# New order of loads, strips, Toeplitz transfers and input products in the state-space stage of a hybrid trunk

## Chip, cores and metric

One NeuronCore of a Trainium2 chip runs the whole program, in float32. The metric is the device time of one execution in microseconds (us), median of the runs; lower is better.

## What is computed

Two layers on a sequence of 512 frames of width 1024: an S5 layer (a diagonal complex state space in 64 groups of 16 channels with 64 states each, then a GLU), a SwiGLU network, a retention layer, another SwiGLU network and a last RMSNorm. The change lies in the first stage alone, which is this part of the reference:

```python
def s5_mixer(u, lam_re, lam_im, log_step, b_re, b_im, c_re, c_im, d, glu_w, glu_b):
    lam = lax.complex(lam_re, lam_im)
    lam_bar = jnp.exp(lam * jnp.exp(log_step)[:, None])
    b_bar = ((lam_bar - 1.0) / lam)[..., None] * lax.complex(b_re, b_im)
    bu = jnp.einsum('blgn,gpn->blgp', uf, b_bar)
    _, states = lax.associative_scan(_linear_recurrence_combine, (a, bu), axis=1)   # a: lam_bar
    y = jnp.einsum('gnp,blgp->blgn', c, states).real + d * uf
    y = jax.nn.gelu(y.reshape(bsz, seq, D_MODEL))
    return y * jax.nn.sigmoid(y @ glu_w + glu_b)

x = x + s5_mixer(rmsnorm(x, s5_norm[j]), ...)     # then: x = x + swiglu(rmsnorm(x), ...)
```

## The kernel before

The program is written out by hand for each engine: a stream of instructions for SyncE (SP), which issues DMAs, and for TensorE (PE), ScalarE (ACT), VectorE (DVE) and GpSimd (POOL), tied by semaphores. Each engine takes its own stream strictly in order, so an instruction that waits holds all that stand behind it. PSUM has eight banks. Each use of a bank is a "fill"; the list `S5_FILLS` (line 79) deals the fills of the stage to banks 4 to 7 in turn, and the consumers wait for `bank_full` and `bank_free` by it. ACT copies nearly every filled bank to SBUF.

The S5 stage works in chunks of 8 steps (64 chunks of 8 steps make the 512 frames; 32 pairs of groups, `J`).

1. SP loads the eigenvalues, B (`b_loaded`), the norm gain, C (`c_loaded`, eight DMAs, line 425), the gain and D on few partitions (`d_loaded`), and six vectors (`vecs_loaded`). ACT issues two DMAs of 1 MB each with x by chunks (`xc_loaded`, line 864).
2. DVE works out the eigenvalues and their powers 0 to 8 (`powers`), then the output powers `c_powers`. ACT copies the gained B into `fb` (four copies), squares the eight steps of x (line 880), takes the root, copies C out of PSUM and writes the normed x (`xn`, line 891).
3. `half_tables` (DVE, line 1248) makes eight half tables for the inputs, three operations of 1024 elements each; PE transposes each (`s5_tables`, line 506); ACT copies it out. PE transposes `xn` (`s5_steps`, line 558) and multiplies tables and inputs (`s5_inputs`, eight results `b`). ACT copies these into `states`.
4. POOL multiplies C by the powers into `r_tc`, seven blocks of it (`tc_ready`); DVE makes the eighth (`tc_last_ready`). From each, PE makes a strip of the convolution (`strips(k)`, line 570); ACT copies it into `strip`, which lies in the space of the raw weights (`w_raw`). DMAs shift copies of the strips into the Toeplitz matrices `toep` (`toeplitz_half(queue, part, half)`, line 389: eight DMAs each; four parts, each of two halves; part p needs strips 2p and 2p+1). Toeplitz memory is zeroed by ACT first.
5. DVE scans the states: within segments (`seg_done` 1), over the segments' carries (`seg_done` 2), and lifts them in four parts (`scan_done` 1 to 4).
6. SP loads x again by tokens (`x_tok`, 2 MB, line 441). PE transposes it to `xT` (line 609), which ACT copies out in eight tiles.
7. PE accumulates `y_inputs(k)` (Toeplitz matrix by inputs, line 639) and `y_states(k)` (line 620) in eight banks. ACT applies the GELU, PE transposes back (`y_transposed`), DVE and ACT copy and split into a high and a low part. The GLU's matmuls follow (lines 673 to 675), and with them the long rest of the program, in which PE is nearly always at work on weights that are split into `w_hi` (ACT) and `w_lo` (DVE).

In the kernel before, ACT issues the second halves of parts 1, 2 and 3, and SP the rest. ACT's split of the first GLU weights, `split_weights(0, 0)`, stands ahead of its eight DMAs of part 3. The PE stream of that point reads:

```python
            pe.wait_ge(seg_done, 2)
            for k in range(4):
                if k % 2 == 0:
                    pe.wait_ge(toep_loaded[k // 2], 16 * 2 * STEPS)
                y_inputs(k)
            strips(6)
            pe.wait_ge(toep_loaded[2], 16 * 2 * STEPS)
            y_inputs(4)
            y_inputs(5)
            keep_clock(s5_open("y", 6)[0], 8)
            for k in range(4):
                y_states(k)
            pe.wait_ge(toep_loaded[3], 16 * 2 * STEPS)
```

Of the kernel before, what the change touches and what calls it, by code (L numbers as in the profile page):

```python
# [30 lines left out]
ALU = mybir.AluOpType  # L31
ACT = mybir.ActivationFunctionType
# [45 lines left out]
SHARED = 4  # L78
S5_FILLS = [("bt", 0), ("bt", 1), ("lam", 0), ("ms", 0), ("vec", 0), ("ct", 0), ("ct", 1)]
S5_FILLS += [("tb", 0), ("tb", 1)] + [("u", k) for k in range(8)] + [("tb", 2), ("tb", 3)]  # L80
for _c in range(1, 4):
    S5_FILLS += [("tb", 4 * _c), ("tb", 4 * _c + 1), ("b", 2 * _c - 2)]
    if _c == 2:
        S5_FILLS += [("strip", 0)]
    S5_FILLS += [("tb", 4 * _c + 2), ("tb", 4 * _c + 3), ("b", 2 * _c - 1)]
S5_FILLS += [("b", 6), ("b", 7), ("strip", 1), ("strip", 7), ("strip", 2), ("strip", 3)]
S5_LATE = [("strip", 4), ("strip", 5), ("strip", 6)]
S5_AT, _used = {}, [0] * 8


def _place(fill, b):
    S5_AT[fill] = (b, _used[b])
    _used[b] += 1
# [8 lines left out]
for _kind in ("y", "yt"):  # L102
    for _k in range(8):
        _place((_kind, _k), _k)
PART = 2 * JB
# [52 lines left out]
def trunk(nc, x, s5_norm, lam_re, lam_im, log_step, b_re, b_im, c_re, c_im, s5_d, glu_w, glu_b,  # L158
          ret_norm, ret_w, ret_gn, ret_wo, ffn_norm, ffn_gate, ffn_up, ffn_down, final_norm,
          ident_in, rope_in, decay_in, out):  # L160
    with ExitStack() as ctx:
# [3 lines left out]
        def sem(name):  # L165
            return ctx.enter_context(nc.semaphore(name))
# [45 lines left out]
        tb = r_w[:, 1024:3072].rearrange("p (r a) -> p r a", r=2)  # L212
        tc_tmp = r_w[:, 0:512]
        prod = r_w[:, 2048:3072].rearrange("p (s a) -> p s a", s=2)
# [9 lines left out]
        rows = r_3[0:J, 4096:4096 + 28 * P].rearrange("p (s a) -> p s a", a=P)  # L224
        vec_rows = r_3[64:64 + NVEC, 4096:4096 + P]
        gain_wide = r_3[:, 8192 - J * N:8192]
# [92 lines left out]
        gain_loaded = sem("gain_loaded")  # L319
        ct_copied = sem("ct_copied")  # L320
        tc_last_ready = sem("tc_last_ready")
# [80 lines left out]
        def _(sp):  # L402
# [17 lines left out]
            for half in range(2):  # L420
                gain_half = s5_norm[0][half * J * N:(half + 1) * J * N]
                sp.dma_start(gain_wide[64 * half:64 * half + 64, :], gain_half.partition_broadcast(64)).then_inc(gain_loaded, 16)
            for ri, src in enumerate((c_re, c_im)):
                for b in range(4):
                    sp.dma_start(c_rows[:, ri, b, :].rearrange("m (h p) -> m h p", h=2),
                                 src[0].rearrange("(h b j) n p -> b (j n) h p", h=2, b=4)[b]).then_inc(c_loaded, 16)
# [5 lines left out]
            for col, vec in ((V_GLU_B, glu_b[0]), (V_RET, ret_norm[0]), (V_FFN0, ffn_norm[0]),  # L432
                             (V_FFN1, ffn_norm[1]), (V_FINAL, final_norm), (V_GN, ret_gn[0])):
                n = vec.shape[0] // P
                sp.dma_start(vec_rows[col:col + n, :], vec.rearrange("(k p) -> k p", p=P)).then_inc(vecs_loaded, 16)

            b, fill = S5_AT[("tb", 4 * NTAB - 1)]
            sp.wait_ge(bank_full[b], fill + 1)
            sp.wait_ge(tb_ready, 2 * NTAB)
            sp.wait_ge(tc_last_ready, 1)  # L440
            sp.dma_start(x_tok, x[0].rearrange("(t p) d -> p t d", p=P)).then_inc(x_loaded, 16)

            toeplitz_half(sp, 0, 0)
            toeplitz_half(sp, 0, 1)
            toeplitz_half(sp, 1, 0)
            toeplitz_half(sp, 2, 0)
            for part in range(2):
# [44 lines left out]
        def _(pe):  # L492
# [54 lines left out]
            pe.matmul(ps[:, 0:STEPS], pair, small[:, 0:STEPS], start=True, stop=True).then_inc(full, 1)  # L547
            ps, full = s5_open("vec", 0)
            pe.wait_ge(vecs_loaded, 6 * 16)
            pe.transpose(ps[:, 0:NVEC], vec_rows, ident[64:64 + NVEC, 64:64 + NVEC]).then_inc(full, 1)  # L550
            pe.wait_ge(c_loaded, 8 * 16)
# [12 lines left out]

            s5_tables(0, 0)
            pe.wait_ge(xn_ready, STEPS)
            for k in range(8):
                s5_steps(k)
            s5_tables(0, 1)
            def strips(k):  # L570
# [14 lines left out]
            for c in range(1, NTAB):  # L585
                s5_tables(c, 0)
                if c == 1:
                    for n in range(8):
                        b, fill = S5_AT[("u", n)]
                        pe.wait_ge(bank_free[b], fill + 1)  # L590
                s5_inputs(2 * c - 2)
                if c == 2:
                    pe.wait_ge(fb_ready, 4)
                    pe.wait_ge(diag_ready, 1)
                    strips(0)
                s5_tables(c, 1)
                s5_inputs(2 * c - 1)
            s5_inputs(NBLK - 2)
            s5_inputs(NBLK - 1)
            strips(1)  # L600
            strips(NBLK - 1)
# [37 lines left out]
            def y_inputs(k):  # L639
                s5_open("y", k)  # L640
                for jj, half, rows64, o in y_pairs(k):


                    pe.matmul(o, u[:, jj, half, :], toep[:, J * half + jj, :], start=(jj % 4 == 0), stop=False)

            pe.wait_ge(seg_done, 2)
            for k in range(4):
                if k % 2 == 0:
                    pe.wait_ge(toep_loaded[k // 2], 16 * 2 * STEPS)
                y_inputs(k)  # L650
            strips(6)
            pe.wait_ge(toep_loaded[2], 16 * 2 * STEPS)
# [189 lines left out]
        def _(act):  # L842
# [24 lines left out]
            act.activation(rows[:, 11, :], rows[:, 10, :], ACT.Sin).then_inc(sin_ready, 1)  # L867
            act.activation(rows[:, 12, :], rows[:, 10, :], ACT.Sin, scale=0.5).then_inc(sin_ready, 1)
            act.wait_ge(fb_zeroed, 1)
            for ri in range(2):  # L870
                b, fill = S5_AT[("bt", ri)]
                act.wait_ge(bank_free[b], fill + 1)
                for half in range(2):
                    rows64 = slice(64 * half, 64 * half + 64)
                    copy(fb[rows64, ri, :, N * half:N * half + N], bt_gained[ri][rows64]).then_inc(fb_ready, 1)
            act.wait_ge(xc_loaded, 32)
            for t in range(STEPS):
                if t:
                    act.wait_ge(ms_ready, t)
                act.activation(junk, xc[:, t, :], ACT.Square, accum_out=small[:, t:t + 1]).then_inc(ms_ready, 1)  # L880
            ps, free = s5_full("ms", 0)
            act.activation(small[:, 8:16], ps[:, 0:STEPS], ACT.Sqrt, bias=eps[:, :], scale=1.0 / D).then_inc(free, 1)
            ps, free = s5_full("vec", 0)
            copy(vecs[:, :], ps[:, 0:NVEC]).then_inc(free, 1)
            for ri in range(2):
# [32 lines left out]

            s5_table_out(0, 0)
            for k in range(8):  # L920
                s5_steps_out(k)
            s5_table_out(0, 1)
            for c in range(1, NTAB):
                s5_table_out(c, 0)
                s5_input_out(2 * c - 2)
                if c == 2:
                    strip_out(0)
                if c == NTAB - 1:
                    zero_toeplitz(2)
                s5_table_out(c, 1)  # L930
                s5_input_out(2 * c - 1)
                if c < NTAB - 1:
                    zero_toeplitz(c - 1)
                else:
                    act.wait_ge(tb_ready, 2 * NTAB)
                    for ri in range(2):
                        copy(ct_last[:, ri, :, :], ct[:, ri, J - JB:J, :]).then_inc(ct_copied, 1)
            s5_input_out(NBLK - 2)
            s5_input_out(NBLK - 1)
            strip_out(1)  # L940
            zero_toeplitz(3)
            strip_out(7)
            for k in range(4, 8):
                zero_toeplitz(k)
            strip_out(2)
            strip_out(3)
            toeplitz_half(act, 1, 1)
            for k in range(KT):
# [3 lines left out]
            strip_out(5)  # L952
            toeplitz_half(act, 2, 1)
            strip_out(6)
            split_weights(0, 0)
            toeplitz_half(act, 3, 1)
# [16 lines left out]
            for k in range(8):  # L973
                gelu(k)
                if k >= 5 and k % 2:
                    y_high((k - 5) // 2)
# [127 lines left out]
        def _(dve):  # L1104
# [115 lines left out]

            step(dve.memset(powers[:, 0, 0, :], 1.0))
            step(dve.memset(powers[:, 1, 0, :], 0.0))
# [13 lines left out]
            for have in (1, 2, 4):  # L1236
# [4 lines left out]

            t = [prod[:, i, :].rearrange("p (r k j) -> p r k j", r=2, k=STEPS) for i in range(2)]
            complex_mul([c_powers[:, i, :, :] for i in range(2)], powers[:, :, 0:STEPS, :],
                        [repeated(lam_t[:, 2 + i, :], 1, STEPS) for i in range(2)], t)
            dve.tensor_copy(seg_powers[:, :, 0, :], powers[:, :, STEPS, :]).then_inc(powers_ready, 1)
            dve.wait_ge(powers_ready, 1)

# [22 lines left out]

            dve.wait_ge(ct_copied, 2)
            js = slice(J - JB, J)
# [332 lines left out]
        def _(pool):  # L1605
# [19 lines left out]

            pool.wait_ge(powers_ready, 1)
            pool.wait_ge(d_loaded, 64)
            d_flat = d_diag[:, :, :].rearrange("p j n -> p (j n)")
# [81 lines left out]
```

## Time and profile before

| | |
|---|---|
| median of 3 runs | 1310.13 us (1308.87 to 1310.64) |
| the profiled execution | 1309.56 us, of which the span is 1307.8 us |
| PE busy | 1253.6 us |
| first GLU matmul (end of the S5 stage) | 123.5 us after the start of the span |

The span runs from the first to the last instruction; 1.8 us lie around it. All times below that look like "89.70" are us from the start of the span. A row of the timeline has start, duration, engine, line, operation, output and inputs, the count, and in brackets the idle time of that engine ahead of it with what ended it. "ACTq" and "SPq" are the queues in which these engines issue DMAs.

### The profile page before, as it was taken

To read this page: it belongs to the slowest core of one execution; us is meant where nothing else is said; L and a number is where in the kernel's file an instruction comes from. 1 tells how busy PE (TensorE), PEld (TensorE's weight loads), DVE (VectorE), ACT (ScalarE), POOL (GpSimd) and SP (SyncE) were. 2 spreads that over 40 slices of the span, in tenths; PEclk is the share of its full clock that TensorE was granted. 3 is DMA by queue.
4 is the path that set the end of the run, shared out by engine and by line. 5 is a ranking of instruction groups with operands and counts; after the bars stand their busy time and mean duration, and the time that the engine had idled before them with its cause. 6 is when DMAs were issued, how large, how long until landed. Compare 5 with 4: busy or idle time off the path is not lost.

```text
span 1307.8 us, 16043 instructions
## 1 busy us (share of the span) xinstructions
PE 1253.6 (96%) x6253; PEld 1039.9 (80%) x6253; DVE 694.8 (53%) x822; ACT 465.5 (36%) x481; POOL 58.1 (4%) x64
## 2 busy tenths in 40 slices
PE   2779999999999999999999999999999999999997
PEld 2768778888887888888888888888788888887886
DVE  8797874444444445555556464554355454444433
ACT  4834544242423333324223332332233232323222
POOL 2960000000000000000000000000000000000000
PEclk9989999999999999999999999999999999999999
DMA  5053323333322323322313223233332323222231
GB/s 112 2 136 100 96 88 105 96 96 96 96 86 81 96 88 114 103 100 96 105 33 121 79 65 103 65 96 96 97 97 88 104 90 102 90 72 89 88 101 73
DMA packets 147791, 119.18 MB, mean 91 GB/s; under 512 B 12857, under 2 KB 140017, under 8 KB 147761
## 3 DMA queue, kind: packets, MB, share of 16 engines
q1 hardware_dynamic: 143584, 115.78, 28.5%
q10 hardware_dynamic: 4176, 2.98, 1.1%
q8 instruction: 21, 0.34, 0.1%
q14 instruction: 10, 0.07, 0.0%
HBM read 114.29 MB, written 2.10 MB: 89 GB/s over the span
## 4 chain that ended last, share of the span: by engine, by line
PE 89%; DVE 4%; ACT 3%; issue 1%; DMA 1%; ACTq 1%; SPq 0%; DVEq 0%
PE bank L673 25%; PE bank L675 25%; PE bank L674 25%; PE bank L769 2%; PE bank L770 2%; PE bank L771 2%; PE bank L780 1%; ACTq L398 1%; DVE w_lo L1126 1%; PE bank L797 1%; PE bank L795 1%; PE bank L796 1%; DVE tmp L1116 1%; DMA w_raw<-in_s_glu_w_dram 1%; PE bank L625 1%
## 5 line engine op out<-in xcount | busy, mean ns | idle before, releaser
L673 PE MATMUL bank<-u_hi,w_hi 128*128 128x512 f32 x960 | 375.5, 391 | 2.0 <-DVE xT L1390 1.1
L675 PE MATMUL bank<-u_hi,w_lo 128*128 128x512 f32 x960 | 374.0, 390 | 0.0
L674 PE MATMUL bank<-u_lo,w_hi 128*128 128x512 f32 x960 | 373.8, 389 | 0.0
L1126 DVE TENSOR_TENSOR w_lo<-w_raw,w_hi 128x2048 fp32r<-128x2048 f32 x112 | 256.7, 2292 | 200.2 <-ACT w_hi L850 199.8
L850 ACT ACTIVATE w_hi<-w_raw 128x2048 fp32r<-128x2048 f32 x112 | 213.5, 1906 | 188.6 <-PE bank L675 146.4
L673 PEld LDWEIGHTS bank<-u_hi,w_hi 128*128 128x128 f32 x960 | 180.3, 188 | 40.5 <-issue 2.0
L675 PEld LDWEIGHTS bank<-u_hi,w_lo 128*128 128x128 f32 x960 | 180.3, 188 | 37.6
L674 PEld LDWEIGHTS bank<-u_lo,w_hi 128*128 128x128 f32 x960 | 180.3, 188 | 37.4 <-issue 0.5
L673 PE MATMUL bank<-h_hi,w_hi 128*128 128x512 f32 x352 | 137.3, 390 | 2.8 <-DVE w_lo L1126 2.8
L674 PE MATMUL bank<-h_lo,w_hi 128*128 128x512 f32 x352 | 137.1, 389 | 0.0
L675 PE MATMUL bank<-h_hi,w_lo 128*128 128x512 f32 x352 | 137.0, 389 | 0.0
L850 ACT ACTIVATE h_hi<-tmp 128x512 f32 x44 | 27.8, 632 | 234.3 <-DVE tmp L1116 234.3
L1116 DVE TENSOR_TENSOR tmp<-bank,tmp 128x512 f32<-128x512 f32 (+3 forms) x60 | 38.1, 635 | 98.9 <-PE bank L675 94.3
L983 ACT ACTIVATE tmp<-xT 128x512 f32 (+1 forms) x32 | 20.2, 633 | 183.4 <-DVE xT L1390 183.4
L673 PEld LDWEIGHTS bank<-h_hi,w_hi 128*128 128x128 f32 x352 | 66.1, 188 | 17.3 <-DVE w_lo L1126 3.6
L674 PEld LDWEIGHTS bank<-h_lo,w_hi 128*128 128x128 f32 x352 | 66.1, 188 | 13.7
L675 PEld LDWEIGHTS bank<-h_hi,w_lo 128*128 128x128 f32 x352 | 66.1, 188 | 13.6
L1390 DVE TENSOR_TENSOR xT<-bank,xT 128x512 f32 (+1 forms) x24 | 16.6, 692 | 96.5 <-PE bank L675 96.5
L1035 ACT ACTIVATE tmp<-tmp 128x512 f32<-128x512 f32 x44 | 27.8, 632 | 70.6 <-DVE tmp L1465 69.6
L1477 DVE TENSOR_TENSOR h_lo<-tmp,h_hi 128x512 f32 x44 | 30.5, 692 | 40.6 <-ACT h_hi L850 40.6
L673 PE MATMUL bank<-y_hi,w_hi 128*128 128x512 f32 x128 | 49.9, 390 | 0.0
L675 PE MATMUL bank<-y_hi,w_lo 128*128 128x512 f32 x128 | 49.8, 389 | 0.0
(199 smaller groups left out, 1352.2 us busy)
## 6 DMA issues: line engine op xcount, KB each, us to landing
w_raw<-in_ret_w_qkvg_dram SPq DMA_DIRECT2D x24, 1024.0 KB, 5.0
w_raw<-in_ffn_w_gate_dram SPq DMA_DIRECT2D x22, 1024.0 KB, 5.1
w_raw<-in_ffn_w_up_dram SPq DMA_DIRECT2D x22, 1024.0 KB, 5.1
w_raw<-in_ffn_w_down_dram SPq DMA_DIRECT2D x32, 704.0 KB, 4.2
w_raw<-in_ret_w_o_dram SPq DMA_DIRECT2D x8, 1024.0 KB, 5.1
w_raw<-in_s_glu_w_dram SPq DMA_DIRECT2D x4, 1024.0 KB, 6.0
s<-in_x_dram ACTq DMA_DIRECT2D x2, 1024.0 KB, 12.2
s_w<-in_x_dram SPq DMA_DIRECT2D x1, 2048.0 KB, 10.0
```

The source lines that it names most:

```text
L673: pe.matmul(o, w_hi[w][:, w_cols], hi, start=first, stop=False)
L674: pe.matmul(o, w_hi[w][:, w_cols], lo, start=False, stop=False)
L675: return pe.matmul(o, w_lo[w][:, w_cols], hi, start=False, stop=end)
L769: pe.matmul(o, a_hi, w_hi[s][:, cols], start=(kk == 0), stop=False)
L770: pe.matmul(o, a_hi, w_lo[s][:, cols], start=False, stop=False)
L771: mm = pe.matmul(o, a_lo, w_hi[s][:, cols], start=False, stop=(kk == KT - 1))
L850: return act.activation(o, i, ACT.Copy, scale=scale)
L983: act.activation(sq, tile(xT, t), ACT.Square).then_inc(sq_ready, 1)
L1035: act.activation(sig[:, m, :], sig[:, m, :], ACT.Silu).then_inc(gate_ready, 1)
L1116: return dve.tensor_tensor(o, a, b, ALU.mult)
L1126: dve.tensor_tensor(w_lo[s][:, :], w_raw[:, s, :], w_hi[s][:, :].bitcast(F32), ALU.subtract).then_inc(w_lo_ready[s], 1)
L1477: dve.tensor_tensor(tile(h_lo, i * 2 + m), act_raw[:, m, :], tile(h_hi, i * 2 + m).bitcast(F32), ALU.subtract).then_inc(h_split, 1)
```

## The change

It changes the order of work inside the S5 stage; nothing that is computed is left out or added.

- SP waits for x by chunks (`xc_loaded`) ahead of its loads of C; all that stands behind these waits too.
- ACT squares x ahead of its copies into `fb`.
- DVE no longer makes `c_powers` and the copy `seg_powers`; POOL does. DVE, not ACT, copies `ct_last`.
- PE transposes the half table (0,1) ahead of the eight transposes of `xn`; ACT's copies follow that order. Strip 1 comes after table 2 rather than after the last inputs; the vectors' transpose comes late.
- The load of x by tokens no longer waits for `tc_last_ready` (the buffer `tc_tmp` moved), but stands behind the 16 DMAs of Toeplitz part 0.
- SP issues parts 0, 1 and 2 whole and the first half of part 3; ACT only the second half of part 3.
- ACT's `split_weights(0, 0)` comes after its second GELU.
- `y_inputs(0)` and `(1)` take banks 2 and 3 and wait only for `seg_done` 1; strip 6 comes between them and `y_inputs(2)`.

```diff
-S5_FILLS = [("bt", 0), ("bt", 1), ("lam", 0), ("ms", 0), ("vec", 0), ("ct", 0), ("ct", 1)]
-S5_FILLS += [("tb", 0), ("tb", 1)] + [("u", k) for k in range(8)] + [("tb", 2), ("tb", 3)]
+S5_FILLS = [("bt", 0), ("bt", 1), ("lam", 0), ("ms", 0), ("ct", 0), ("ct", 1)]
+S5_FILLS += [("tb", k) for k in range(4)] + [("u", k) for k in range(8)]
...
+Y_BANK = [2, 3, 0, 1, 4, 5, 6, 7]
...
-        tc_tmp = r_w[:, 0:512]
+        tc_tmp = xT[:, 7, :]
...
+            sp.wait_ge(xc_loaded, 32)
             for ri, src in enumerate((c_re, c_im)):
...
+            toeplitz_half(sp, 0, 0)
+            toeplitz_half(sp, 0, 1)
+
             b, fill = S5_AT[("tb", 4 * NTAB - 1)]
             sp.wait_ge(bank_full[b], fill + 1)
             sp.wait_ge(tb_ready, 2 * NTAB)
-            sp.wait_ge(tc_last_ready, 1)
             sp.dma_start(x_tok, x[0].rearrange("(t p) d -> p t d", p=P)).then_inc(x_loaded, 16)
 
-            toeplitz_half(sp, 0, 0)
-            toeplitz_half(sp, 0, 1)
-            toeplitz_half(sp, 1, 0)
-            toeplitz_half(sp, 2, 0)
+            for part in range(1, NPART - 1):
+                for half in range(2):
+                    toeplitz_half(sp, part, half)
...
             s5_tables(0, 0)
+            s5_tables(0, 1)
             pe.wait_ge(xn_ready, STEPS)
             for k in range(8):
                 s5_steps(k)
-            s5_tables(0, 1)
...
+            pe.wait_ge(seg_done, 1)
+            pe.wait_ge(toep_loaded[0], 16 * 2 * STEPS)
+            y_inputs(0)
+            y_inputs(1)
+            strips(6)
             pe.wait_ge(seg_done, 2)
-            for k in range(4):
-                if k % 2 == 0:
-                    pe.wait_ge(toep_loaded[k // 2], 16 * 2 * STEPS)
-                y_inputs(k)
-            strips(6)
+            pe.wait_ge(toep_loaded[1], 16 * 2 * STEPS)
+            y_inputs(2)
+            y_inputs(3)
...
-            toeplitz_half(act, 1, 1)
             for k in range(KT):
...
             strip_out(5)
-            toeplitz_half(act, 2, 1)
             strip_out(6)
-            split_weights(0, 0)
             toeplitz_half(act, 3, 1)
...
                 gelu(k)
+                if k == 1:
+                    split_weights(0, 0)
...
             pool.wait_ge(powers_ready, 1)
+            b, fill = S5_AT[("lam", 0)]
+            pool.wait_ge(bank_free[b], fill + 1)
+            t = [xT[:, i, :].rearrange("p (r k j) -> p r k j", r=2, k=STEPS) for i in range(2)]
+            for i in range(2):
+                step(mul(t[i], powers[:, :, 0:STEPS, :],
+                         repeated(repeated(lam_t[:, 2 + i, :], 1, STEPS), 1, 2)))
+            settle()
+            step(pool.tensor_tensor(c_powers[:, 0, :, :], t[0][:, 0], t[1][:, 1], ALU.subtract))
+            pool.tensor_tensor(c_powers[:, 1, :, :], t[0][:, 1], t[1][:, 0], ALU.add).then_inc(c_powers_ready, 1)
```

## Rows read from the trace of the kernel before

**Rows 1.** The page's first part: busy time, share of the span, instructions of PE.

```profile
PE 1253.6 (96%) x6253; PEld 1039.9 (80%) x6253; DVE 694.8 (53%) x822; ACT 465.5 (36%) x481; POOL 58.1 (4%) x64
```

**Rows 2.** Chain that ended last, 60 to 125 us: start, duration, what.

```profile
89.70 0.56 SPq L398
...
94.90 7.79 DMA w_raw<-in_s_glu_w_dram
...
107.30 2.77 DMA s<-w_raw
```

**Rows 3.** Timeline of PE, 79 to 124 us.

```profile
79.67 4.90 PE L609 MATMUL bank<-ident,s_w 128*128 128x128 f32 x24 [2.99 <-ACT xT L850]
...
86.71 1.94 PE L578 MATMUL bank<-s_tc,s_fb 128*32 128x128 f32 x16
...
97.39 1.97 PE L644 MATMUL bank<-s,s_u 128*64 128x128 f32 x32 [1.62 <-DMA s<-w_raw]
...
101.27 7.53 PE L625 MATMUL bank<-s_tc,s_states 64*64 64x128 f32 x128
110.11 1.97 PE L644 MATMUL bank<-s,s_u 128*64 128x128 f32 x32 [1.31 <-DMA s<-w_raw]
...
123.53 0.48 PE L673 MATMUL bank<-g_hi,w_hi 128*128 128x512 f32 x1
```

**Rows 4.** Stretches: length, busy time of each engine, granted clock, DMA share, GB/s.

```profile
68.00:72.00 4.00, 3.95 (x45) 3.42 (x43) 3.86 (x5) 4.00 (x6) 3.76 (x5) 1.00 1.01 407
...
72.00:75.30 3.30, 0.00 (x0) 0.00 (x0) 3.16 (x5) 0.88 (x2) 3.22 (x3) 1.00 0.92 196
...
79.60:82.80 3.20, 3.13 (x14) 2.76 (x15) 3.10 (x4) 1.88 (x5) 3.04 (x4) 0.50 0.34 70
```

**Rows 5.** Line 864 (x by chunks), its landings; DMA queues of 16 to 19 us.

```profile
DMA to landing us min/median/max: 9.9/12.2/14.5
...
q1 hardware_dynamic: 1644, 0.42, 75.5%
q10 hardware_dynamic: 148, 0.27, 43.1%
```

**Rows 6.** The page's DMA issues (x by tokens); line 398, SP, 79 to 86 us.

```profile
s_w<-in_x_dram SPq DMA_DIRECT2D x1, 2048.0 KB, 10.0
...
L398 SPq DMA_DIRECT2D s<-w_raw x7: 600/605/611, 78.7 to 82.6; - x7
...
DMA to landing us min/median/max: 1.8/2.0/2.3
```

**Rows 7.** Timeline of ACT, 18 to 64 us.

```profile
18.57 2.44 ACT L850 ACTIVATE s_fb<-bank 64x512 f32<-64x512 f32 x4 [8.91 <-DVE bank L1116]
...
27.05 1.28 ACT L882 ACT_TABLE_LOAD   x1
...
30.45 5.00 ACT L891 ACTIVATE s<-s,small 128x512 f32<-128x512 f32 x8
...
60.93 1.97 ACT L850 ACTIVATE s_states<-bank 128x512 f32<-128x512 f32 x2
63.80 0.59 ACT L850 ACTIVATE w_raw<-bank 32x512 f32<-32x512 f32 x1 [0.89 <-PE bank L581]
```

**Rows 8.** Timeline of DVE, 22 to 67 us.

```profile
22.49 1.30 DVE L1116 TENSOR_TENSOR s_w<-s_powers,s_lam_t 128x512 f32<-128x512 f32 x2
...
24.84 1.23 DVE L1116 TENSOR_TENSOR bank<-bank,s_powers 128x1024 f32<-128x1024 f32 x1
...
41.63 1.22 DVE L1259 TENSOR_TENSOR s_w<-bank,s_w 128x1024 f32<-128x1024 f32 x1 [3.17 <-PE bank L513]
...
65.85 1.23 DVE L1116 TENSOR_TENSOR bank<-s_states,bank 128x1024 f32<-128x1024 f32 x1
```

**Rows 9.** Timeline of POOL, 30 to 87 us.

```profile
30.80 2.17 POOL L1616 TENSOR_TENSOR s_pool_tmp<-s_ct,s_c_powers 128x512 f32<-128x512 f32 x2
...
85.00 1.27 POOL L1670 TENSOR_TENSOR s_tc<-s_pool_tmp 128x512 f32<-128x512 f32 x1
```

More of the change, by code:

```diff
@@ L78 @@
 SHARED = 4
-S5_FILLS = [("bt", 0), ("bt", 1), ("lam", 0), ("ms", 0), ("vec", 0), ("ct", 0), ("ct", 1)]
-S5_FILLS += [("tb", 0), ("tb", 1)] + [("u", k) for k in range(8)] + [("tb", 2), ("tb", 3)]
+S5_FILLS = [("bt", 0), ("bt", 1), ("lam", 0), ("ms", 0), ("ct", 0), ("ct", 1)]
+S5_FILLS += [("tb", k) for k in range(4)] + [("u", k) for k in range(8)]
 for _c in range(1, 4):
[L82 to L86, printed above, removed]
+    for _h in range(2):
+        S5_FILLS += [("tb", 4 * _c + 2 * _h), ("tb", 4 * _c + 2 * _h + 1), ("b", 2 * _c - 2 + _h)]
+        if _c == 2:
+            S5_FILLS += [("strip", _h)]
+S5_FILLS += [("b", 6), ("b", 7), ("vec", 0), ("strip", 7), ("strip", 2), ("strip", 3)]
 S5_LATE = [("strip", 4), ("strip", 5), ("strip", 6)]
+Y_BANK = [2, 3, 0, 1, 4, 5, 6, 7]
 S5_AT, _used = {}, [0] * 8
@@ L103 @@
     for _k in range(8):
-        _place((_kind, _k), _k)
+        _place((_kind, _k), Y_BANK[_k])
 PART = 2 * JB
@@ L224, in trunk @@
         rows = r_3[0:J, 4096:4096 + 28 * P].rearrange("p (s a) -> p s a", a=P)
-        vec_rows = r_3[64:64 + NVEC, 4096:4096 + P]
+        vec_rows = xT[64:64 + NVEC, 6, 0:P]
         gain_wide = r_3[:, 8192 - J * N:8192]
@@ L319, in trunk @@
         gain_loaded = sem("gain_loaded")
-        ct_copied = sem("ct_copied")
+        c_powers_ready = sem("c_powers_ready")
         tc_last_ready = sem("tc_last_ready")
@@ L547, in _ @@
             pe.matmul(ps[:, 0:STEPS], pair, small[:, 0:STEPS], start=True, stop=True).then_inc(full, 1)
-            ps, full = s5_open("vec", 0)
-            pe.wait_ge(vecs_loaded, 6 * 16)
-            pe.transpose(ps[:, 0:NVEC], vec_rows, ident[64:64 + NVEC, 64:64 + NVEC]).then_inc(full, 1)
             pe.wait_ge(c_loaded, 8 * 16)
@@ L597, in _ @@
                 s5_inputs(2 * c - 1)
+                if c == 2:
+                    strips(1)
             s5_inputs(NBLK - 2)
             s5_inputs(NBLK - 1)
-            strips(1)
+            ps, full = s5_open("vec", 0)
+            pe.wait_ge(vecs_loaded, 6 * 16)
+            pe.transpose(ps[:, 0:NVEC], vec_rows, ident[64:64 + NVEC, 64:64 + NVEC]).then_inc(full, 1)
             strips(NBLK - 1)
@@ L868, in _ @@
             act.activation(rows[:, 12, :], rows[:, 10, :], ACT.Sin, scale=0.5).then_inc(sin_ready, 1)
+            act.wait_ge(xc_loaded, 32)
+            for t in range(STEPS):
+                if t:
+                    act.wait_ge(ms_ready, t)
+                act.activation(junk, xc[:, t, :], ACT.Square, accum_out=small[:, t:t + 1]).then_inc(ms_ready, 1)
             act.wait_ge(fb_zeroed, 1)
@@ L875, in _ @@
                     copy(fb[rows64, ri, :, N * half:N * half + N], bt_gained[ri][rows64]).then_inc(fb_ready, 1)
[L876 to L880, printed above, removed]
             ps, free = s5_full("ms", 0)
             act.activation(small[:, 8:16], ps[:, 0:STEPS], ACT.Sqrt, bias=eps[:, :], scale=1.0 / D).then_inc(free, 1)
-            ps, free = s5_full("vec", 0)
-            copy(vecs[:, :], ps[:, 0:NVEC]).then_inc(free, 1)
             for ri in range(2):
@@ L919, in _ @@
             s5_table_out(0, 0)
+            s5_table_out(0, 1)
             for k in range(8):
                 s5_steps_out(k)
-            s5_table_out(0, 1)
             for c in range(1, NTAB):
-                s5_table_out(c, 0)
-                s5_input_out(2 * c - 2)
+                for ri in range(2):
+                    s5_table_out(c, ri)
+                    s5_input_out(2 * c - 2 + ri)
+                    if c == 1:
+                        zero_toeplitz(ri)
+                    if c == 2:
+                        strip_out(ri)
                 if c == 2:
-                    strip_out(0)
-                if c == NTAB - 1:
                     zero_toeplitz(2)
[L930 to L937, printed above, removed]
             s5_input_out(NBLK - 2)
             s5_input_out(NBLK - 1)
-            strip_out(1)
+            ps, free = s5_full("vec", 0)
+            copy(vecs[:, :], ps[:, 0:NVEC]).then_inc(free, 1)
             zero_toeplitz(3)
             strip_out(7)
+            strip_out(2)
+            strip_out(3)
             for k in range(4, 8):
                 zero_toeplitz(k)
-            strip_out(2)
-            strip_out(3)
-            toeplitz_half(act, 1, 1)
             for k in range(KT):
@@ L1219, in complex_mul @@
                 settle()
-            step(dve.memset(powers[:, 0, 0, :], 1.0))
             step(dve.memset(powers[:, 1, 0, :], 0.0))
@@ L1240, in _ @@
                             powers[:, :, 1:have + 1, :], top, t)
[L1242 to L1246, printed above, removed]
+            dve.memset(powers[:, 0, 0, :], 1.0).then_inc(powers_ready, 1)
             def half_tables(c, ri):
@@ L1269, in _ @@
                         dve.reciprocal(small[:, 16:24], small[:, 8:16]).then_inc(rs_ready, 1)
-            dve.wait_ge(ct_copied, 2)
+            for ri in range(2):
+                step(dve.tensor_copy(ct_last[:, ri, :, :], ct[:, ri, J - JB:J, :]))
+            settle()
+            dve.wait_ge(c_powers_ready, 1)
             js = slice(J - JB, J)
@@ L1626, in _ @@
             pool.wait_ge(powers_ready, 1)
+            b, fill = S5_AT[("lam", 0)]
[4 more added lines that the diff above has]
+                         repeated(repeated(lam_t[:, 2 + i, :], 1, STEPS), 1, 2)))
+            settle()
+            step(pool.tensor_tensor(c_powers[:, 0, :, :], t[0][:, 0], t[1][:, 1], ALU.subtract))
+            pool.tensor_tensor(c_powers[:, 1, :, :], t[0][:, 1], t[1][:, 0], ALU.add).then_inc(c_powers_ready, 1)
+            step(pool.tensor_copy(seg_powers[:, :, 0, :], powers[:, :, STEPS, :]))
+            settle()
+            pool.wait_ge(c_powers_ready, 1)
             pool.wait_ge(d_loaded, 64)
```

## The prediction

> **What bounds the kernel now.** I read the page first: PE is busy 1253.6 of 1307.8 us [rows 1]. From the first GLU matmul at 123.53 [rows 3] it hardly stops, and nothing after it is touched, so the change is worth what it moves that matmul, one for one. So the chain of waits of the S5 stage comes next. It is not a chain of arithmetic but of transfers: at 89.70 SP starts eight Toeplitz DMAs, at 94.90 it loads the first GLU weights, for 7.79 us; only then may ACT split them, and only behind that issue its last eight DMAs, of which the last starts at 107.30 and takes 2.77 us [rows 2]. PE waits for that at 110.11, from where 13.4 us of y work lead to the GLU [rows 3]. The timelines of PE, ACT, DVE and POOL give the durations, the stretches give the clock.
>
> The number to find is when `y_inputs(6)` and `(7)` end. Before it is 110.11 + 1.9 = 112.0. Two things lead there now: Toeplitz part 3 (110.1), and PE's own line: part 2 in place at 97.39, two `y_inputs` and the clock keeper (3.9 us, to 101.27), four `y_states` (7.5 us, to 108.8) [rows 3]. The second is only 1.3 us ahead of the first.
>
> **Start.** Of the two loads of x by chunks the slower lands 14.5 us after its issue [rows 5], at about 18.9. In 16 to 19 us the SP queue, with C and what follows, took 75.5% of 3 us, 2.3 us of all engines' time, beside x [rows 5]. With C held back I take that off: x at 16.6 (bounds 18.9, nothing gained, and 15.9). ACT then squares (27.05 - 21.0 = 6.0 us, 21.0 being where the `fb` copies end) and copies `fb` (2.44) [rows 7]: 25.1. DVE is free earlier, at 22.49, where `c_powers` began, but its tables wait for `fb`: they start at 25.1 instead of 24.84 [rows 8]. What POOL gains costs nothing: two products at 1.1 (2.17 for two), two sums between 0.6 and 1.3 (the 1.27 of a sum twice as wide, by half or whole), of which I take 0.8, so 4.1 us with the copy, from 22.6; then D at about 29.4, where it formerly began its blocks at 30.80 [rows 9]. Its last block ends at 85.0 instead of 86.3. The C loads land at about 23, and their transposes are wanted by ACT at 26.7.
>
> ACT's `xn` starts when the first table and the reciprocal are through, 25.1 + 3.8 = 28.95 instead of 30.45 [rows 7].
>
> **Tables to scan.** DVE lost 3.17 us waiting for the transpose of table (0,1), which stood behind those of `xn` [rows 8]. It now goes first, so the stall goes, and the tables end at 54.4 instead of 57.5. Next late is ACT, which has the copies. Its last `b` ended at 62.9, 32.4 us after `xn` began [rows 7]. In the new order it gives away the 0.4 us of `ct_last` and, as I follow it, 0.6 of its waits for PE, and takes strip 1, 0.6: 32.0 from 28.95, so 61. The scan starts there instead of 65.85 [rows 8]. DVE's own last block of `r_tc` is done at 59 and hides. So `seg_done` 1 comes at about 80, 2 at 85, the last `scan_done` at 102; all are ahead of their use, as below. The 4.8 us won here lie off the path.
>
> **Strips, x, Toeplitz.** Following PE and ACT through the new order of banks, strip 1 is copied at 54.0; before it was 63.80 + 0.59 [rows 7]. SP then issues 16 DMAs at 0.64 us (0.605 and a gap) [rows 6]: 10.2 us, to 64.2, and only then the load of x by tokens, before issued at 65.3. It landed in 10.0 us [rows 6], sharing the engines with Toeplitz transfers all the while. Now part 0 is out ahead of it and part 1 joins only at 67.5. 2.1 MB at the 407 GB/s of 68 to 72 us [rows 4], plus the 1.8 to 2.0 that the smallest DMAs take [rows 6], are 7.0; between 7.0 and 10.0 I take 8.5: 72.7.
>
> PE is through strip 3 at 66.9 and idles 5.8 us. In the trace, 3.3 us of idle before 75.33 brought the granted clock from 1.00 to 0.50, the 1.2 GHz level, and it rose again after 3.2 us of work [rows 4]. The eight x tiles start at half clock: 0.9 us each for 3.2 us, then 0.6 (24 transposes, six tiles, took 4.90 with both) [rows 3]: 6.0 us, to 78.7. ACT no longer stands still for its DMAs of part 1. Strips 4 and 5 take 2.2 each (the tiles end at 84.5, strip 5 begins at 86.71) [rows 3], the copy 0.6: 83.7 instead of 89.6. This is a gain of 5.9 us.
>
> Most of it is paid back: part 2 was issued by two queues at once, eight each, in 5.1 us from 89.70 [rows 2]; now SP issues all 16. The last starts 15 x 0.643 = 9.65 us after the first, at 93.4, and lands in 2.0 (the median of SP's there, 1.8 to 2.3 [rows 6]; the last of ACT's took 2.77 [rows 2]). So part 2 is in place at **95.4** instead of 97.39: 2.0 us earlier. The wait on it holds all of PE's line.
>
> **The end of the stage.** PE has done `y_inputs` 0 to 3 and strip 6 by 89.4 (strip 6 waits for POOL's 85.0), and then idles 6.0 us. In the kernel before the corresponding gap was 1.62 [rows 3], and the clock stayed at 1.00. A gap of 3.3 let it fall [rows 4], so I expect it at 0.50 here; 3.2 us at half clock cost half of that, 1.6. "TensorE: Matmul & The Clock Gate" of the Trainium skill (section "Loop structure matters more than you think") likewise says that a long DMA wait between matmuls lets the clock drop; the trace agrees with its 0.50.
>
> From 95.4: 3.9, then 7.5, then 1.9, with no wait before the last, plus 1.6: **110.3**, against 112.0. Part 3 is no longer in the way: ACT issues its half from 88.1, SP its own behind the GLU weights, from 94.1 to 99.5, and all is in place by 103. The wait of 1.3 us before 110.11 is gone. ACT's `split_weights(0, 0)` is hidden too: weights at 102, the second GELU at 105.2, `w_hi` to 107.1, DVE's `w_lo` 2.3 more, 109.4, ahead of the first `y_copy` at 110.8. That cover is 1.4 us thick. From 110.3 to the GLU nothing changes (11.5 us).
>
> **Sum.** 2.0 (part 2) + 1.3 (wait gone) - 1.6 (clock) = 1.7 us. The profiled execution, 1309.56, becomes 1307.9; the median, 0.57 above it, 1308.4.
>
> **Rivals.**
>
> *A, the clock holds or comes back at once, or x lands quickly.* Without the 1.6 the gain is 3.3 (1306.8); with x in 7.0 us as well 4.8 (1305.3). For it: nothing in the rows shows a gap of exactly this sort, and PE has been at work for 10 us ahead. Against it: the gap is nearly twice the one that made it fall.
>
> *B, slower: the clock fails twice and x is late.* Place: from the x tiles to `toep_loaded[2]`. If x takes 10.0 us as before (+1.5), the tiles all run at 0.9 (+1.2), and the strips start at half clock (+1.6), part 2 comes at 99.7, and the end at 114.6: 2.6 us later, 1312.7. It decides from part 2 at 99.7 on; at 97.1 nothing is gained or lost. For it: SP issues everything in one row, so all of this adds up. Against it: the clock rose during x tiles, at 82.8, 3.2 us after they resumed [rows 4].
>
> The Trainium skill, in the same page (section "Part 4: PE-mode transpose"), says that transposes don't count as work for the clock. By that rule the tiles would stay at half clock throughout, which is the middle term of B; the trace speaks against it, with the rise at 82.8 amid transposes.
>
> *C, holding back C brings x nothing.* If x still lands at 18.9, tables, strips and transfers are all 2.3 us later: 1.7 - 2.3 = -0.6, 1310.7. For it: the two queues' shares of 16 to 19 us add up to 119% [rows 5], so one does not simply displace the other. Against it: the 2.3 us that C takes in 16 to 19 us.
>
> **How the numbers follow.** My forecast has 0.46, C 0.15, A 0.27, B 0.12. A measurement of this kernel tells about 0.2%, 2.6 us, from no change: below 1307.5 or above 1312.7. A is faster (0.27), B slower (0.12), the rest within (0.61). The range goes from between A's two values to between C and B, 1306.0 to 1311.9; the unknown terms (x landing +-1.5, start -0.7 to +2.3) fit in it.
>
> **What would show it.** Tables at about 25 and no stall of DVE in them; the scan at 61; x by tokens landing near 72.7; sixteen SP issues from 83.7 without a break; PE idle about 6 us before its `y_inputs(4)` at 95.4, then clock 0.50 for 3 us; no wait ahead of `y_inputs(6)`; first GLU matmul at 121.8. I am wrong if part 2 is in place before 94 or after 97, or if the stretches after it show 1.00.

## The result, and the profile after

| kernel | median, us | to the kernel before, with 95% interval | first GLU matmul, us |
|---|---|---|---|
| before | 1309.89 (11 runs) | | 123.53 |
| changed | 1313.30 (11 runs) | 1.0028 [1.0019, 1.0037] | 128.07 |

The change makes the kernel slower by 0.28% (0.19 to 0.37%); its median lies above the 1312.7 from which I had said that I would call it slower. I had forecast 1308.4, with a range up to 1311.9: wrong in sign and outside the range. The time beyond the first GLU matmul is 1312.4 - 128.07 = 1184.3 us of the span after and 1307.8 - 123.53 = 1184.3 before. So all of it comes from the S5 stage, one for one, as expected. In the two profiled executions the stage is 4.5 us longer; the medians are 3.4 us apart, and the sums below are those of the two executions. One execution of the kernel before, among those beside the experiments, took 5438.71 us and is left out of the ratios as slow.

SP's queue in the changed kernel (timeline: start, duration, engine, line, operation, output and input, count; L399 issues the Toeplitz DMAs, L445 the load of x by tokens, L408 that of the GLU weights):

```profile
18.41 1.94 SPq L427 DMA_DIRECT2D s_states<-in_s_c_re_dram  x4
...
55.78 12.20 SPq L399 DMA_DIRECT2D s<-w_raw  x16
68.08 0.54 SPq L445 DMA_DIRECT2D s_w<-in_x_dram  x1
68.73 31.73 SPq L399 DMA_DIRECT2D s<-w_raw  x32
100.55 0.54 SPq L408 DMA_DIRECT2D w_raw<-in_s_glu_w_dram  x1
```

The load of x by tokens is issued at 68.08, behind the 16 Toeplitz DMAs of part 0; before, it went out at 65.28. PE's timeline, from the transposes of the normed x on:

```profile
36.30 5.57 PE L561 MATMUL bank<-ident,s 128*128 128x128 f32 x32
...
77.56 4.26 PE L613 MATMUL bank<-ident,s_w 128*128 128x128 f32 x20 [9.56 <-DMA s_w<-in_x_dram]
...
83.92 1.94 PE L578 MATMUL bank<-s_tc,s_fb 128*32 128x128 f32 x16
...
86.14 1.94 PE L578 MATMUL bank<-s_tc,s_fb 128*32 128x128 f32 x16
...
101.70 3.58 PE L648 MATMUL bank<-s,s_u 128*64 128x128 f32 x32 [7.27 <-DMA s<-w_raw]
105.20 2.05 PE L507 MATMUL bank<-ident 128*128 128x128 f32 x16
107.19 7.53 PE L629 MATMUL bank<-s_tc,s_states 64*64 64x128 f32 x128
114.65 1.97 PE L648 MATMUL bank<-s,s_u 128*64 128x128 f32 x32
```

Two gaps stand out, both ended by a DMA: 9.56 us ahead of the x tiles (3.38 before), and 7.27 us ahead of `y_inputs(4)`, against 1.62 before [rows 3]. Part 2 is in place at 101.70 instead of 97.39. The 16 products of `y_inputs(4)` and `(5)` that follow (x32: the rows count each float32 product twice, and each transpose once) take 3.58 us; they took 1.97 [rows 3]. The 1.31 us ahead of `y_inputs(6)` [rows 3] are gone. So 4.3 (part 2) + 1.6 (the slow products) - 1.3 = 4.6 us, the whole loss between these two executions. The stretches of the second gap and after it show the clock (length, then the busy time of PE, PE load, DVE, ACT and POOL, the granted clock, DMA share, GB/s):

```profile
94.40:101.70 7.30, 0.03 (x2) 0.00 (x1) 6.99 (x15) 1.28 (x1) 0.00 (x0) 0.76 0.51 85
101.70:105.30 3.60, 3.60 (x33) 3.38 (x33) 1.59 (x4) 0.00 (x0) 0.00 (x0) 0.54 0.95 310
105.30:107.20 1.90, 1.90 (x17) 1.78 (x18) 0.00 (x0) 0.00 (x0) 0.00 (x0) 1.00 0.71 122
```

The chain of waits that leads to the second gap's end runs from the copy of strip 5 through all 16 of SP's issues of part 2 without another wait (start, duration, what; three of its rows):

```profile
88.46 0.60 ACT w_raw L857
...
89.13 0.56 SPq L399
...
99.84 1.81 DMA s<-w_raw
```

Of the start, the timelines of DVE and ACT show:

```profile
26.78 1.23 DVE L1116 TENSOR_TENSOR bank<-bank,s_powers 128x1024 f32<-128x1024 f32 x1 [4.34 <-ACT s_fb L857]
```
```profile
30.66 5.01 ACT L896 ACTIVATE s<-s,small 128x512 f32<-128x512 f32 x8 [1.36 <-DVE small L1264]
...
55.09 0.59 ACT L857 ACTIVATE w_raw<-bank 32x512 f32<-32x512 f32 x1 [1.14 <-PE bank L581]
```

DVE now waits 4.34 us for `fb`, and `xn` starts at 30.66, no earlier than before (30.45) [rows 7]. Strip 1 is copied at 55.09; before it was 63.80 [rows 7].

### The profile page after: what moved, and what is told of

It reads as the page before. It is cut to its first block, busy times and chain, and to the rows that moved or that the text cites. A ratio compares the mean times of both kernels' runs of the same rounds, so it can differ in the third digit from the quotient of the medians.

```text
span 1312.4 us, 16044 instructions
## 1 busy us (share of the span) xinstructions
PE 1256.7 (96%) x6253; PEld 1042.2 (79%) x6253; DVE 692.8 (53%) x819; ACT 464.3 (35%) x479; POOL 62.3 (5%) x69
## 4 chain that ended last, share of the span: by engine, by line
PE 90%; ACT 3%; DVE 2%; DMA 2%; SPq 1%; issue 1%; ACTq 0%; DVEq 0%
PE bank L680 25%; PE bank L682 25%; PE bank L681 25%; PE bank L778 2%; PE bank L776 2%; PE bank L777 2%; PE bank L787 1%; PE bank L629 1%; SPq L399 1%; DMA s<-in_x_dram 1%; DMA s_w<-in_x_dram 1%; DVE w_lo L1126 1%; PE bank L804 1%; PE bank L803 1%; PE bank L802 1%
## 5 line engine op out<-in xcount | busy, mean ns | idle before, releaser
L681 PEld LDWEIGHTS bank<-h_lo,w_hi 128*128 128x128 f32 x352 | 66.1, 188 | 13.5
L1388 DVE TENSOR_TENSOR xT<-bank,xT 128x512 f32 (+1 forms) x24 | 16.6, 692 | 95.8 <-PE bank L682 95.8
L681 PE MATMUL bank<-y_lo,w_hi 128*128 128x512 f32 x128 | 49.8, 389 | 0.0
```

Of the source, the lines that this page charges most:

```text
L681: pe.matmul(o, w_hi[w][:, w_cols], lo, start=False, stop=False)
```

## Experiments

My account after the result: SP's one line sets the end of the stage, in two places, through x (issued late, behind part 0) and through part 2 (16 issues where two queues took eight each). The rivals: the new start is to blame, or late blocks of POOL, or the slow products have another cause than the clock. POOL is out by the rows of the changed kernel: its last block is done at 85.09, and strip 6, which needs it, begins at 90.25 without a wait. All kernels below but the last of the table are the changed kernel with an edit. The span less the time of the first GLU matmul is 1184.3 to 1184.5 us in every one of them, so that time measures the stage; what differs from one execution of a kernel to the next then seems to arise there too. The last two columns are of one execution each, while the eleven executions of the changed kernel lie between 1311.41 and 1315.42: a difference of 1 or 2 us between two of these profiles can be chance, unless the rows show where it comes from. The runs of the kernel before beside them had medians of 1309.56 (for "start as before", "x first", "part 2 on two queues" and "late split") and 1309.43 (for the rest).

| kernel | median, us | ratio to before, 95% interval | part 2 in place | first GLU matmul |
|---|---|---|---|---|
| changed | 1313.30 | 1.0028 [1.0019, 1.0037] | 101.70 | 128.07 |
| start as before | 1313.13 | 1.0030 [1.0019, 1.0042] | 101.05 | 127.94 |
| x first | 1309.10 | 0.9996 [0.9986, 1.0005] | 95.72 | 122.77 |
| part 2 on two queues | 1305.90 | 0.9971 [0.9961, 0.9982] | 95.23 | 120.00 |
| both | 1301.01 | 0.9935 [0.9921, 0.9948] | by 89.2 | 113.84 |
| changed, gap bridged | 1312.06 (one run) | | 101.12 | 125.89 |
| two queues, no keeper | 1303.57 | 0.9954 [0.9938, 0.9969] | 94.22 | 117.00 |
| both, no keeper | 1299.06 | 0.9921 [0.9908, 0.9935] | 90.26 | 113.04 |
| before, late split | 1308.71 | 1.0000 [0.9990, 1.0009] | 97.62 | 122.39 |

**The start as before.**

```diff
-            sp.wait_ge(xc_loaded, 32)
             for ri, src in enumerate((c_re, c_im)):
...
-            act.wait_ge(xc_loaded, 32)
-            for t in range(STEPS):
-                ...
-                act.activation(junk, xc[:, t, :], ACT.Square, accum_out=small[:, t:t + 1]).then_inc(ms_ready, 1)
             act.wait_ge(fb_zeroed, 1)
             for ri in range(2):
                 ...
+            act.wait_ge(xc_loaded, 32)
+            for t in range(STEPS):
+                ...
+                act.activation(junk, xc[:, t, :], ACT.Square, accum_out=small[:, t:t + 1]).then_inc(ms_ready, 1)
```

> The changed kernel with its start put back: SP doesn't wait for x before it loads C, and ACT copies fb ahead of the squares. My account (the start is one link of the chain): DVE's tables begin near 22.6 instead of 26.78, xn near 29.7 instead of 30.66, strip 1 about 1.0 earlier, first GLU matmul at 126.6 to 127.1 instead of 128.07. Rival (holding C back helps x, and without it all is later): x at 18.9 instead of 18.4 and the first GLU matmul at 128.5 or later.

PE's timeline and one stretch of this kernel:

```profile
35.50 6.22 PE L560 MATMUL bank<-ident,s 128*128 128x128 f32 x32 [2.13 <-ACT s L856]
...
127.94 0.47 PE L679 MATMUL bank<-g_hi,w_hi 128*128 128x512 f32 x1
```
```profile
34.00:40.40 6.40, 4.90 (x23) 4.93 (x24) 6.26 (x6) 5.46 (x11) 6.17 (x6) 0.50 0.00 1
```

DVE's tables do begin at 22.32 instead of 26.78, yet the GLU comes only 0.13 us earlier, and the median is 0.17 us lower: neither my 1.0 to 1.5 nor the rival's loss. Two things eat the 4.5 us. DVE must still wait 2.61 us for the root of the squares ahead of its reciprocal, so `xn` starts at 29.87, only 0.8 earlier. And PE's transposes of `xn` start at 35.50 instead of 36.30 but take 6.22 instead of 5.57 us, with the granted clock at 0.50 through 34.00 to 40.40: in the changed kernel PE was busy between 34.19 and 36.16 with table (0,1), here it had done that early and idled. The two end within 0.2 us of each other (41.7 and 41.9). In the six kernels below that keep the changed start, the clock is at 1.00 from 36 to 42 and the same transposes take 4.46 to 5.79 us. So the new order of the start does not cause the loss, as far as this comparison can tell. Holding C back may have helped x a little: without it the slower load of x by chunks lands 14.5 us after its issue in the kernel before, 15.7 with the late split and 15.9 here; with it, 13.5 to 14.4 in seven kernels.

**x first.**

```diff
-            toeplitz_half(sp, 0, 0)
-            toeplitz_half(sp, 0, 1)
             b, fill = S5_AT[("tb", 4 * NTAB - 1)]
             ...
             sp.dma_start(x_tok, x[0].rearrange("(t p) d -> p t d", p=P)).then_inc(x_loaded, 16)
+            toeplitz_half(sp, 0, 0)
+            toeplitz_half(sp, 0, 1)
```

> The changed kernel with the load of x by tokens ahead of Toeplitz part 0 in SP's line. My account (x behind 16 DMAs makes the x tiles, strips 4 and 5 and part 2 late): x issued near 58 and landed near 67.5, strip 5 then waits for POOL's block at 77.9, part 2 in place at 93 to 95 instead of 101.70, first GLU matmul at 120 to 122 instead of 128.07, 6 to 8 us off the time. Rival (the x tiles are not what holds strips 4 and 5, or part 2's 16 issues alone cost the time): less than 2 us.

SP's queue and PE:

```profile
57.97 0.39 SPq L442 DMA_DIRECT2D s_w<-in_x_dram  x1
58.48 35.56 SPq L399 DMA_DIRECT2D s<-w_raw  x48
```
```profile
72.69 4.70 PE L613 MATMUL bank<-ident,s_w 128*128 128x128 f32 x24 [3.60 <-ACT xT L857]
...
95.72 3.68 PE L648 MATMUL bank<-s,s_u 128*64 128x128 f32 x32 [6.14 <-DMA s<-w_raw]
```

It gains 5.3 us (4.2 between the medians) and brings the kernel back to the time of before. x goes out 10.1 us earlier, but strip 5 is copied only 6.6 earlier (82.45): the tiles now wait 3.60 us for ACT, which zeroes four blocks of Toeplitz memory ahead of its copies (3.87 us from 68.29). Part 2 comes 6.0 earlier: another 0.6 is lost in part 2 itself, two of whose issues took 1.0 us and whose last transfer took 2.25 instead of 1.81. SP's line has hardly a pause left in its 48 issues, 35.56 us: it waited 0.7 us for strip 5. I had expected 6 to 8 and left out both. The gap of 6.14 us and the slow products (3.68) are still there.

**Part 2 on two queues.**

```diff
-            for part in range(1, NPART - 1):
-                for half in range(2):
-                    toeplitz_half(sp, part, half)
+            toeplitz_half(sp, 1, 0)
+            toeplitz_half(sp, 1, 1)
+            toeplitz_half(sp, 2, 0)
...
             strip_out(5)
+            toeplitz_half(act, 2, 1)
             strip_out(6)
```

> The changed kernel with the second half of part 2 on ACT's queue again, as before the change. My account (one line of 16 issues costs 5, and lengthens PE's gap so that the clock falls): part 2 in place at 97 instead of 101.70, granted clock 1.00 in y_inputs(4) and (5) since the gap is 2.6 us instead of 7.3, first GLU matmul near 121.9 instead of 128.07. Rival (transfers are limited by the DMA engines, not by the issuing queue): part 2 within 1.5 us of 101.70.

```profile
95.23 1.97 PE L648 MATMUL bank<-s,s_u 128*64 128x128 f32 x32 [1.79 <-DMA s<-w_raw]
97.12 2.05 PE L507 MATMUL bank<-ident 128*128 128x128 f32 x16
...
120.00 0.47 PE L680 MATMUL bank<-g_hi,w_hi 128*128 128x512 f32 x1
```
```profile
95.20:97.10 1.90, 1.87 (x32) 1.73 (x32) 1.86 (x5) 0.00 (x0) 0.00 (x0) 1.00 1.03 313
```

This one edit turns a loss into a gain: 8.1 us off the stage (7.4 between the medians), 6.5 because part 2 is in place at 95.23, and 1.6 because the gap is now 1.79 us and the products take 1.97 at a clock of 1.00. I had expected 97 and 121.9. Of the 6.5, the second queue gives 5.5: from the copy of strip 5 (ended at 88.05) to part 2 in place it takes 7.2 us, in the changed kernel 12.6 (from 89.05). The other 1.0 is chance: x had landed that much earlier (tiles from 76.40), and nothing ahead of it was changed. The other traces agree. That stretch takes 12.6 to 13.3 us in the four kernels with one queue (changed, start as before, x first, gap bridged) and 7.1 to 7.8 in five with two (before, late split, this one, and the two without the keeper).

The same stretch in the changed kernel and in this one:

```profile
89.10:101.70 12.60, 5.33 (x80) 4.69 (x75) 12.08 (x25) 1.87 (x2) 0.00 (x0) 0.86 0.41 72
```
```profile
88.10:95.20 7.10, 5.34 (x80) 4.70 (x74) 6.75 (x15) 0.59 (x1) 0.00 (x0) 1.00 0.45 103
```

The DMA engines are less than half busy in either (shares 0.41 and 0.45), and part 2 moved by more than the rival's 1.5 us. So the rival, that the engines and not the issuing queue limit the transfers, is out. The kernel is faster than the one before. The Trainium skill, "Trainium Kernel Development and Optimization" (section "Key Constraints"), says that issuing from several engines saves only the sequencer's issue time; the trace agrees, and here that issue time was 5.5 us of the path.

**Both.** The two edits above together.

> The changed kernel with both repairs: the load of x ahead of Toeplitz part 0, and the second half of part 2 on ACT's queue. My account (one line of SP issues is the bottleneck, first through x, then by part 2): the two gains add up partly, part 2 in place near 90, y_states held by the scan parts (scan_done 2 at about 95) rather than by transfers, first GLU matmul at 114.9 to 116.5, about 4 us better than with part 2 on two queues alone (120.00). Rival (once part 2 is on two queues, something else such as POOL's blocks or ACT holds the line): first GLU matmul at 118.5 or later.

Its chain of waits (start, duration, what):

```profile
83.79 1.27 POOL s_tc L1681
...
85.11 1.93 PE bank L578 x16
...
87.39 3.64 PE bank L648 x64
91.04 1.98 PE bank L507 x16
```

The gains are 5.3 and 8.1 alone and 14.2 together (4.2, 7.4 and 12.3 between the medians): they add up, and the 0.9 more than the sum is within what two executions differ by. First GLU matmul at 113.84, 1.1 better than the range I had expected, and not for the reason I gave: what is last now is POOL's seventh block, done at 85.06, with strip 6 behind it, as the rival said, though not at its time. The scan holds nothing: `y_states` start without a wait.

**The gap bridged.** The changed kernel, with

```diff
             y_inputs(3)
+            keep_clock(s5_open("y", 6)[0], 26)
             pe.wait_ge(toep_loaded[2], 16 * 2 * STEPS)
```

> The changed kernel with 26 more clock-keeping products of the identity in the gap of 7.27 us before y_inputs(4); nothing else. My account (the gap drops the clock, at a price of 1.6 us): y_inputs(4) and (5) take 1.97 instead of 3.58 us, part 2 is in place at 101.7 as before, first GLU matmul near 126.4 instead of 128.07. Rival (those matmuls are slow for another reason, such as the glu weights' DMA beside them): they still take 3 us or more.

```profile
101.12 1.97 PE L648 MATMUL bank<-s,s_u 128*64 128x128 f32 x32 [1.77 <-DMA s<-w_raw]
```
```profile
101.10:103.00 1.90, 1.88 (x32) 1.73 (x32) 1.07 (x3) 0.00 (x0) 0.00 (x0) 1.00 0.86 275
```

The same products beside the load of the GLU weights (share 0.86; 0.95 in the changed kernel, and 1.03 with part 2 on two queues, where they take 1.97 as well) take 1.97 instead of 3.58 us once PE has been kept at work. So the clock is the cause, and its price in the changed kernel is 1.6 us. This kernel ran once. The rest of the 2.2 us that this kernel gains is part 2, by chance 0.6 earlier.

**Without the clock keeper.** The kernels with part 2 on two queues, and with both edits, less one line:

```diff
-            keep_clock(s5_open("y", 6)[0], 8)
```

> The changed kernel with the second half of part 2 on ACT's queue and without the eight clock-keeping products ahead of y_states. If the clock holds anyway (gap of 1.79 us), their 2.05 us come off the path whole: first GLU matmul near 118.0 instead of 120.00. Rival (they are needed, or y_states then wait for the scan): first GLU matmul at 119.3 or later.

```profile
94.22 1.97 PE L648 MATMUL bank<-s,s_u 128*64 128x128 f32 x32 [1.78 <-DMA s<-w_raw]
96.11 7.53 PE L629 MATMUL bank<-s_tc,s_states 64*64 64x128 f32 x128
```

With a gap of 1.78 us the keeper isn't needed: `y_states` still take 7.53 us. 117.00 instead of 120.00 is its 2.0, plus part 2 a chance 1.0 earlier; the medians are 2.3 apart.

> Both repairs and no clock-keeping products. My account: where y_states wait for the scan anyway, the 2.05 us of the keeper are hidden or nearly so: within 1.0 us of the kernel with both repairs. Rival (the transfers still set the line there): about 2 us better than it.

```profile
90.26 1.97 PE L648 MATMUL bank<-s,s_u 128*64 128x128 f32 x32 [0.88 <-DMA s<-w_raw]
92.15 7.53 PE L629 MATMUL bank<-s_tc,s_states 64*64 64x128 f32 x128
```

Here part 2 is last again (a wait of 0.88), and the first GLU matmul is 0.8 us earlier than with the keeper. But strip 5 was copied 1.3 us later in this execution (83.12) than in the other (81.85), with the same code up to there. The medians, 1301.01 and 1299.06, are 1.95 apart: that is nearer to the rival's 2 than to my "within 1.0", and the scan, on which I had counted, holds `y_states` in neither. This is the best kernel of the study: 1299.06 us, 0.79% under the one before.

**The late split alone**, put into the kernel before: ACT's `split_weights(0, 0)` goes from ahead of its last Toeplitz half to behind its second GELU.

```diff
             strip_out(6)
-            split_weights(0, 0)
             toeplitz_half(act, 3, 1)
...
                 gelu(k)
+                if k == 1:
+                    split_weights(0, 0)
```

> The kernel before with one part of the change alone: ACT splits the first GLU weights after its second GELU. My account: part 3 is issued from about 96 instead of 102.80, the wait of 1.31 us before y_inputs(6) goes, first GLU matmul at 122.2 instead of 123.53, time 1.3 us less than before (within 0.2%). Rival (the split then delays the first y copies): first GLU matmul at 123.5 or later.

```profile
108.96 1.97 PE L644 MATMUL bank<-s,s_u 128*64 128x128 f32 x32
...
122.39 0.47 PE L673 MATMUL bank<-g_hi,w_hi 128*128 128x512 f32 x1
```

No wait stands ahead of `y_inputs(6)` any more, and the GLU comes 1.1 us earlier, though part 2 was 0.2 later. The mechanism shows in the trace; the runs can't tell the 1.1 us (ratio 1.0000).

## Why the prediction was wrong

The frame held: the chain of transfers sets the stage, part 2's arrival holds all of PE, and from it 13.3 us and the clock's price lead to the end of `y_inputs(7)`. What failed is the arrival itself, 95.4 forecast and 101.70 measured: the sum of SP's issues, the load of x behind them and the start. Its terms, in order (the first two are contained in the third; from there they add up to 6.3):

| step | forecast | measured | error |
|---|---|---|---|
| x by chunks lands | 16.6 | 18.4 | 1.8 |
| `xn` starts | 28.95 | 30.66 | 1.7 |
| strip 1 copied, SP may start | 54.0 | 55.7 | 1.7 |
| 16 issues of part 0, to the issue of x | 10.2 | 12.4 | 2.2 |
| x by tokens, issue to landing | 8.5 | 9.5 | 1.0 |
| eight x tiles | 6.0 | 6.4 | 0.4 |
| strips 4 and 5, copied | 5.0 | 5.1 | 0.1 |
| part 2, first issue to landing | 11.7 | 12.6 | 0.9 |
| part 2 in place | 95.4 | 101.7 | 6.3 |

Of the 6.3, SP's issues were mis-sized by 3.1 (2.2 in part 0, 0.9 in part 2), the start by 1.7, x in flight by 1.0.

- **Start.** x at 18.4, not 16.6. I subtracted the share of the C transfers from the landing of x as if it had displaced x one for one. It had not: the two queues' shares of 16 to 19 us added up to 119% [rows 5], which I named and set aside (my rival C, given 0.15, said 2.3 us; 1.8 came true). The old order of the start would not have won this back: with tables 4.5 us earlier the end moved by 0.13, as a wait for the root and the half clock in the transposes took it back. What an x that really lands at 16.6 would be worth, no run shows.
- **Issues.** I took 0.64 us each from seven issues that ran smoothly [rows 6]. Of the 16 of part 0, two were long:

```profile
L399 SPq DMA_DIRECT2D s<-w_raw x1: 1265/1265/1265, 57.8 to 57.8; - x1
...
L399 SPq DMA_DIRECT2D s<-w_raw x1: 1683/1683/1683, 61.8 to 61.8; - x1
```

  The rows that group all of SP's issues in the kernel before would have told (timeline, and line 398 with its shortest, median and longest issue in ns):

```profile
65.78 29.01 SPq L398 DMA_DIRECT2D s<-w_raw  x32
```
```profile
L398 SPq DMA_DIRECT2D s<-w_raw x40: 551/605/1444, 65.8 to 101.6; - x40
```

  Less the 6.4 us that SP waited in it for strip 5, that is 0.71 each, and the longest of all 40 took 1.44. The 16 of part 0 cost 12.2, not 10.2, and part 2's took 10.7 instead of 9.65 from the first to the last issue.
- **x in flight.** 9.5, nearer to the 10.0 of before than to a low end that I had put together from a rate and a latency and that no row had shown. In the experiments the same load took 8.6 to 10.2.
- **Clock.** Right: 0.54 over the products after the gap (101.70 to 105.30), a price of 1.6 us, as forecast. The bridged gap shows it. In "start as before" and "x first", with the same sort of gap, the slow stretch reached into the keeper too (2.47 and 2.63 us for its 2.05), a price of 2.1 and 2.3 us. One row I had read loosely: ahead of 75.33 in the kernel before, the clock was at 1.00 through the whole gap and until 76.0, and fell as the tiles ran; the 2.99 us of idle after it followed at 0.50.
- **Part 3 and the split of the weights.** Right: no wait ahead of `y_inputs(6)`, and DVE's `w_lo` hidden.
- **The scan.** It starts at 62.40 instead of 65.85, off the path, as said, if later than 61.

So the mechanisms were the right ones and their sum had the wrong sign: the terms follow each other in one line, so that their errors add, and nearly each was taken at or near its best row. The profit that I counted at strip 5, 5.9 us, was 0.6 (copied at 89.05, before at 89.62); the price of the single queue remained: 12.6 us from strip 5 to part 2 in place, where two queues had taken 7.8 (89.62 to 97.39). My rival B had the place (part 2 from 99.7 on) and nearly the time, 1312.7, but from a clock that fails in the tiles; the tiles took 6.4 us, and the real lateness was SP's.

What stays open: why single issues take 1.3 to 1.7 us. In each of the stretches 57 to 58 and 61 to 62 an instruction queue moved a packet of 0.02 MB (SP's data queue had shares of 51.5% and 20.9% there), and the long issues of the kernel before (1.44 us at 69.8) and of "x first" (1.72 us at 80.1) have such a packet within a microsecond too. But an issue of 1.54 us at 72.7 in the changed kernel has none beside it. It is a coincidence in the traces, and no run here tests it.

## What to carry to other kernels

Count a queue's issues as work of an engine: 16 of these DMAs in one line took 10.7 and 11.6 us before the last one started, and what is issued behind them, here a 2 MB load that PE needs soon, is late by as much. If the second queue's engine has the time, split a group of DMAs on which one wait stands over two queues (5.5 us here), and put the large load that is wanted first ahead of the many small ones. When several terms of a sum lie in one line, their errors add; take each from the row that contains the bad cases too.

## What the runs showed of the hardware

- PE's clock can swallow a gain upstream: with its tables 4.5 us earlier, PE idled 2.13 us ahead of the transposes of `xn`, the granted clock was at 0.50 (1.2 GHz) from 34.00 to 40.40, and 32 transposes took 6.22 us instead of 5.57 (4.46 to 5.79 in six more kernels at 1.00).
- The clock rose during transposes (in the tiles of the kernel before, at 82.8: 0.50 up to there [rows 4], 0.98 from 82.80 to 84.50); the rule of the Trainium skill that they don't count ("TensorE: Matmul & The Clock Gate", section "Part 4: PE-mode transpose") doesn't hold for the float32 transposes of this kernel.
- Eight products of the identity, meant to keep the clock up, cost 2.0 us of the path and bring nothing where the gap ahead is 1.8 us: without them `y_states` still take 7.53 us.
- The same 16 small DMAs and their landing took 12.6 to 13.3 us from one queue and 7.1 to 7.8 from two, with the DMA engines busy 0.41 and 0.45 of the time.
